# Stage A's low weights: VectorE's difference replaced by an accumulating transfer

## What is computed

```python
h = rmsnorm(x, pre_norm_g[0])
p = h @ w_in                           # (2112, 1024) @ (1024, 3072)
a, g, z = jnp.split(p, 3, axis=-1)
c = a * jax.nn.sigmoid(g)              # then a causal depthwise convolution of 31 taps over c
y = silu(layernorm(conv(c))) * silu(z)
x = x + rmsnorm(y @ w_out, post_norm_g[0])
```

## Time and profile before

| | |
|---|---|
| median of 3 runs | 2333.99 us (2333.13 to 2339.67) |
| the profiled execution | 2334.64 us |
| its span, first to last instruction | 2332.9 us |
| mean granted clock of TensorE | 0.991 |
| stage A in the span | about 24 to 600 us |
| chain that ended last | PE 91%, DMA 3%, DVE 3%, ACT 1%, POOL 1% |
| VectorE, ACT, POOL busy | 1644.4, 921.3, 246.0 us |

### The profile page before, as it was taken

The page is one execution under the profiler, slowest core; times in us unless marked ns, Lnnn a source line. Parts: engine busy times, 40 slices in busy tenths (PEclk is TensorE's granted clock), DMA queues, the critical chain, the costliest instruction groups (busy, mean ns, idle before and its releaser), DMA issues.

```text
span 2332.9 us, 30211 instructions
## 1 busy us (share of the span) xinstructions
PE 2264.9 (97%) x12020; PEld 1972.4 (85%) x12020; DVE 1644.4 (70%) x2044; ACT 921.3 (39%) x1385; POOL 246.0 (11%) x419
## 2 busy tenths in 40 slices
PE   7899999999999998999998999999999999998998
PEld 6788899999888886888886888877879999996885
DVE  5589999997578988989888937742376666665221
ACT  5422222222443224666664115531136565655110
POOL 1100000101221100000000101210110000000000
PEclk9999999999999999999999999999999999999999
DMA  4322333323545313333335335342213232326221
GB/s 168 122 91 93 115 121 135 111 85 120 152 155 180 109 46 110 97 108 118 119 113 227 108 138 213 134 161 80 81 59 103 93 101 95 97 84 247 84 106 37
DMA packets 126075, 275.18 MB, mean 118 GB/s; under 512 B 17136, under 2 KB 53488, under 8 KB 124144
## 3 DMA queue, kind: packets, MB, share of 16 engines
q1 hardware_dynamic: 102448, 194.61, 25.7%
q0 software_dynamic: 23488, 78.64, 8.8%
HBM read 194.82 MB, written 78.75 MB: 117 GB/s over the span
## 4 chain that ended last, share of the span: by engine, by line
PE 91%; DMA 3%; DVE 3%; ACT 1%; issue 1%; POOL 1%; SPq 0%; DVEq 0%; ACTq 0%
PE PS L1966 29%; PE PS L1967 29%; PE PS L1968 29%; PE PS L2164 2%; DMA s_scratch<-m 1%; DMA st<-s_scratch 1%; PE PS L2034 1%; PE PS L2012 1%; DMA yb<-y_scratch 1%; PE PS L1977 1%; DMA raw<-wa_in_in 0%; DVE xn L1376 0%; PE PS L2021 0%; DVE Wbl L1371 0%; DMA xt<-x_in 0%
## 5 line engine op out<-in xcount | busy, mean ns | idle before, releaser
L1405 DVE SCALAR_TENSOR_TENSOR acc<-cp,cw,acc 128x513 f32<-128x513 f32 (+3 forms) x464 | 360.4, 777 | 13.7
L1966 PE MATMUL PS<-HAh,Wh 128*128 128x512 f32 (+2 forms) x960 | 341.5, 356 | 0.1
L1967 PE MATMUL PS<-HAl,Wh 128*128 128x512 f32 (+2 forms) x960 | 339.6, 354 | 0.0
L1968 PE MATMUL PS<-HAh,Wl 128*128 128x512 f32 (+2 forms) x960 | 339.4, 354 | 0.0
L1966 PE MATMUL PS<-Wbh,s7h 128*128 128x512 f32 (+1 forms) x544 | 216.2, 398 | 21.3 <-DVE Wbl L1371 21.3
L1967 PE MATMUL PS<-Wbl,s7h 128*128 128x512 f32 (+1 forms) x544 | 213.9, 393 | 0.0
L1968 PE MATMUL PS<-Wbh,s7l 128*128 128x512 f32 (+1 forms) x544 | 213.5, 392 | 0.0
L1966 PE MATMUL PS<-Vh,HBh 128*128 128x512 f32 (+1 forms) x544 | 212.4, 390 | 0.1
L1967 PE MATMUL PS<-Vl,HBh 128*128 128x512 f32 (+1 forms) x544 | 211.8, 389 | 0.0
L1968 PE MATMUL PS<-Vh,HBl 128*128 128x512 f32 (+1 forms) x544 | 211.7, 389 | 0.0
L1966 PEld LDWEIGHTS PS<-HAh,Wh 128*128 128x128 f32 x960 | 181.2, 189 | 15.5 <-issue 0.5
(11 more groups left out here) (198 smaller groups left out, 5112.4 us busy)
## 6 DMA issues: line engine op xcount, KB each, us to landing
raw<-wa_in_in SPq DMA_DIRECT2D x48, 512.0 KB, 3.6
rawv<-wb_v_in SPq DMA_DIRECT2D x64, 256.0 KB, 4.8
QWr<-wb_uz_in SPq DMA_DIRECT2D x64, 256.0 KB, 2.6
v_scratch<-vb POOLq DMA_DIRECT2D x64, 256.0 KB, 2.6
vt<-v_scratch SPq DMA_DIRECT2D x32, 512.0 KB, 3.7
s_scratch<-m POOLq DMA_DIRECT2D x32, 512.0 KB, 3.8
rawb<-wb_out_in SPq DMA_DIRECT2D x32, 512.0 KB, 5.9
st<-s_scratch SPq DMA_DIRECT2D x14, 1024.0 KB, 4.9
```

The source lines that it names most:

```text
L1405: return nc.vector.scalar_tensor_tensor(out=out, in0=src, scalar=w, in1=first, op0=ALU.mult, op1=ALU.add)
L1966: nc.tensor.matmul(out, wh, xh, start=start, stop=False, skip_group_check=seeded)
L1967: nc.tensor.matmul(out, wh, xl, start=False, stop=False, skip_group_check=seeded)
L1968: return nc.tensor.matmul(out, wl, xh, start=False, stop=stop, skip_group_check=seeded)
```

## The change

VectorE's `a_low` goes. ACT, right after `Wh`, writes `Wl = -Wh` (a second copy with scale -1, which first waits for the one before). POOL then issues a transfer from the weights in DRAM into `Wl` that adds to what is there, so that `Wl` ends as weights minus `Wh`. It has semaphores of its own, one for each of the three buffers, and TensorE waits for those. On POOL the transfers for units 0, 1 and 2 stand behind the powers of tiles 3, 5 and 7, and the one for unit n + 2 behind the powers of turn n of the unit loop, ahead of that turn's stores. SP's load of `raw` stays as it was, so the weights are read twice.

```diff
+        a_lo = [sem(f"a_lo{i}") for i in range(3)]
+        a_hi, a_neg, a_mm, a_sig, a_prod, a_zs = (sem(f"a_{n}") for n in ("hi", "neg", "mm", "sig", "prod", "zs"))
...
+            def a_low(n):
+                pool.wait_ge(a_neg, n + 1)
+                nc.gpsimd.dma_start(kp(Wl[n % 3]), wa_in[n % UNITS_A, :, :], accum_op=ALU.add).then_inc(a_lo[n % 3], 16)
...
             for t in range(9):
                 n1_rsqrt(t)
+                if t in (3, 5, 7):
+                    a_low(t // 2 - 1)
             for n in range(2 * UNITS_A):
                 h, j, m = unit_a(n)
                 for i in (2 * n, 2 * n + 1):
                     if 9 + i < NTILES:
                         n1_rsqrt(9 + i)
+                if 3 <= n + 2 < 2 * UNITS_A:
+                    a_low(n + 2)
                 if m == 1:
                     c_store(JA * h + j)
...
             def a_high(n):
                 act.wait_ge(a_raw[n % 3], 16 * (n // 3 + 1))
                 nc.scalar.activation(kp(Wh[n % 3]), kp(raw[n % 3]), ACT.Copy).then_inc(a_hi, 1)
+
+                act.wait_ge(a_hi, n + 1)
+                nc.scalar.activation(kp(Wl[n % 3]), kp(Wh[n % 3]).bitcast(fp32), ACT.Copy, scale=-1.0).then_inc(a_neg, 1)
...
-            def a_low(n):
-                dve.wait_ge(a_hi, n + 1)
-                split_low(kp(Wl[n % 3]), kp(raw[n % 3]), kp(Wh[n % 3]), a_lo)
...
                 if c == (1 if n < 3 else 0):
-                    if 3 <= n + 2 < 2 * UNITS_A:
-                        a_low(n + 2)
...
                 n1_low(t)
-                if t in (1, 3, 5):
-                    a_low(t // 2)
...
                 if c == 0:
-                    pe.wait_ge(a_lo, n + 1)
+                    pe.wait_ge(a_lo[n % 3], 16 * (n // 3 + 1))
```

More of the change, by code:

```diff
@@ L335, in build @@
         a_raw = [sem(f"a_raw{i}") for i in range(3)]
-        a_hi, a_lo, a_mm, a_sig, a_prod, a_zs = (sem(f"a_{n}") for n in ("hi", "lo", "mm", "sig", "prod", "zs"))
+        a_lo = [sem(f"a_lo{i}") for i in range(3)]
+        a_hi, a_neg, a_mm, a_sig, a_prod, a_zs = (sem(f"a_{n}") for n in ("hi", "neg", "mm", "sig", "prod", "zs"))
         a_cst, a_zst, a_tap, a_conv = (sem(f"a_{n}") for n in ("cst", "zst", "tap", "conv"))
```

## The result

| | before | after |
|---|---|---|
| median | 2335.95 us (4 runs) | 2366.3 us (4 runs, 2362.63 to 2367.07) |
| profiled execution: span | 2332.9 us | 2365.3 us |
| mean granted clock of TensorE | 0.991 | 0.986 |

The ratio is 1.0127, with a 95% interval of 1.0115 to 1.0139: 30 us slower by both, and the sum of the forecast is 29.

What follows compares the result with a forecast made beforehand. Stage A was taken as bound by TensorE from about 105 us, before that by the row-statistics chain. Start delay, transfer waits and clock losses, less old waits, gave +29.1 us on 2334.6: 2364, range 2353 to 2390.

Steps and rivals of the forecast that it cites:

- unit 2, start of chunk 2: Stage A's start: unit 2's transfer, behind tile 7's power, lands at 43.0 against a 38.1 start; +4.9 us, copy's 1.1 included.
- clock behind chunk 2: After the new wait at chunk 2, TensorE restarts at the lower granted clock; +1.7 us, likewise at chunk 6.
- wait at chunk 6: Unit 3's transfer, queued on POOL behind tile 12's power, makes TensorE wait 5.7 + 5.5 - 0.9 = 10.3 us.
- wait at chunk 8: Unit 4's transfer, queued on POOL behind tile 14's power, makes TensorE wait 3.0 + 5.5 = 8.5 us.
- wait at chunk 10: Unit 5's transfer, queued on POOL behind tile 16's power, makes TensorE wait 8.5 us.
- landing L: Adding transfer's time from issue to landing, estimated at 5.5 us from plain transfers; possible from 3.2 to 9.1.
- The 4.4 us: Alternative landing estimate for the 512 KB adding transfer, from the Trainium skill's pages; it would make the sum 4.4 us less.
- the transfer is cheap: Rival: landing about 3.2 us, the waits short, +20 us, 2355; chance 0.82 together with the forecast.
- rival A: Adding transfer much slower than a plain one, above 9 us; 2399 at 12 us; chance 0.13, shared with a split-up add.
- rival B: POOL runs ahead at units 3, 4 and 5 and only old waits go: 2334, at best 2332; chance 0.05.
- ACT's copy: ACT's second copy, about 1.1 us each, costs only at stage A's start, ahead of tile 3's square: +1.1 us.
- the old waits: Waits of 4.2 and 3.1 us before the transposes of tiles 13 and 15 vanish in longer ones; 0.8 comes back.

Runs made afterwards that it cites:

- the reordered queue: The first follow-up: changed kernel with adding transfers for units 0 to 6 moved ahead of powers in POOL's queue; 2346.4 us, ratio 1.0036 to the kernel before.
- the last and fastest kernel: Kernel before with raw loads for units 5, 6 ahead of loads of tiles 14, 16, and first store of c ahead of tile 12's power; 2326.1 us.
- SP's new order: Kernel before with SP's loads of raw for units 5 and 6 issued ahead of the loads of tiles 14 and 16; 2329.4 us, ratio 0.9971.

## Why the prediction was right

It was right in sign and mechanism: four waits for the adding transfer, at the chunks and behind the powers that it names. The time came out within 3 us (2366.3 against 2364), and that is in part luck, as the table shows. Times are counted from the first transposes, which start at 9.80 in the execution after and at 8.35 in the one before, 1.45 us later, as gpre landed after 6.7 us there and 5.3 here:

| step | predicted | traced |
|---|---|---|
| VectorE's difference gone | 0 | 0 (0.9999 with it alone) |
| unit 0: start of the first chunk | +1.1 | 26.13 - 23.78 - 1.45 = +0.9 |
| unit 2, start of chunk 2 | +4.9 | 45.34 - 38.10 - 1.45 = +5.8 |
| clock behind chunk 2 | +1.7 | 9.93 - 7.24 = +2.7 |
| wait at chunk 6 | 10.3 | 10.27 |
| clock behind it | +1.7 | 22.64 - 9.93 - 10.27 = +2.4 |
| tile 13: old wait, what comes back | -4.2, +0.8 | -4.2, +0.63 |
| wait at chunk 8 | 8.5 | 8.69 |
| tile 15: old wait | -3.1 | -3.3 |
| wait at chunk 10 | 8.5 | 8.70 |
| clock behind chunks 8 and 10, over that of before | 0 | +0.5, +0.7 |
| sum at the transposes of tile 16 | +29.1 | 139.68 - 105.29 - 1.45 = +32.9 |
| landing L | 5.5 | 5.6 |

(9.93, 7.24 and 22.64 are the differences of the two timelines at 72.57 and 62.64, at 45.34 and 38.10, and at 91.62 and 68.98.) Rows of the kernel before and then of the kernel after, for chunk 0 and the end of the stretch:

```profile
30.10 1.91 PE L1977 MATMUL PS<-con,xn 128*128 128x128 f32 x16
...
68.98 1.03 PE L1977 MATMUL PS<-con,xn 128*128 128x128 f32 x8
...
105.29 0.70 PE L1977 MATMUL PS<-con,xn 64*128 64x64 f32 x8
```
```profile
33.77 1.91 PE L1981 MATMUL PS<-con,xn 128*128 128x128 f32 x16
...
139.68 0.71 PE L1981 MATMUL PS<-con,xn 64*128 64x64 f32 x8
```

So the sum was 3.8 us short in the stretch that it describes, the later start added 1.45, and some 2 us were given back behind stage A (34.4 us at tile 16, 32.4 in the spans), 1.6 of them in the wait for y_scratch, 1.0 for 2.6. Together they leave the difference of the spans 3 us from the sum, and that of the medians, 30.3, 1 us.

**The waits** at chunks 6, 8 and 10 came out within 0.2 us each, because their first part could be read before: the place in POOL's queue from a store that stood there already. The landing was a luckier sum. 4.3 for a plain transfer and 1.3 for twice the bytes make 5.6; measured are 3.8 for the plain one and 1.8 for the add, 5.6 as well. The 4.4 us that stands beside it in the prediction as an estimate, with the 4.4 us lower sum, is not what the trace shows: 5.6 decides. The range's lower part (the transfer is cheap) was excluded by the landing of 5.6, rival A by the same, rival B by the four waits. VectorE's busy time fell by 52.5 us and not by 59, ACT's rose by 50.8.

**Chunk 2** came 0.9 us later than the sum had it, and more than that is in chunk 0: it takes 33.77 - 26.13 = 7.64 us in the kernel after and 30.10 - 23.78 = 6.32 before. Its matmuls start 0.43 us apart at first and 0.23 later on; after ten such gaps in one trace and after three in the other. The change is not shown to be the reason. The same count is 0 with ACT's copy alone, 3 in the reordered queue and 9 in the last and fastest kernel. The windows show a granted clock of 1.00 there all the same.

**The clock** was under-sized, at 1.7 us for a restart. Windows of the kernel after behind chunk 6:

```profile
84.00:86.00 2.00, 2.00 (x5) 1.61 (x6) 0.00 (x0) 0.00 (x0) 0.00 (x0) 0.50 1.02 416
86.00:88.00 2.00, 2.00 (x6) 1.52 (x6) 0.00 (x0) 1.28 (x1) 0.00 (x0) 0.50 0.92 279
88.00:90.00 2.00, 2.00 (x9) 1.66 (x8) 0.00 (x0) 0.00 (x0) 0.00 (x0) 0.86 0.44 178
```

1.0 + 1.0 + 0.3 = 2.3 us. The 1.7 was read off one execution, and one is not enough: TensorE's wait of 8.12 us for sz (at 910.72 in the trace of before) is the same to 0.01 us in ten of the eleven traces, and the windows behind it show 1.7 us (with the plain transfer) to 3.1 (in the kernel after) lost at the lower level, 1.2 GHz; the kernel before has 2.8. A price for a restart that is read off one row can be off by over 1 us.

**ACT's copy** was the step with the weakest reasoning, though it hardly moved the sum. "It costs where ACT is in the chain, which is at the start: +1.1" is right only because the waits for Wl cover the rest; the copies in the turns of chunks 5 and 6 had been counted in the 5.7 and the 7.1, as they should. By itself the copy, with the difference waiting for it, costs 5 to 6 us. The same is true of the old waits: I took 4.2 and 3.1 off as given back, which is right, and concluded for the first experiment that they would come back in part, which is wrong; they came back in full and with the copy on top (5.7 and 4.2, and 5.7 and 3.3 with the copy alone). The changed kernel was predicted well because its own waits were the longest in the stretch; the kernels between it and the one before weren't.

## What to carry to other kernels

A transfer or a store in a queue that works in program order is as late as the latest thing ahead of it: ask for each item what it waits for, and whether the items behind need that too. Read the lateness of a new item off an old one in the same place. Before a wait is explained by what the change adds, look whether the same wait is in the kernel before and what it hangs on. And where several waits lie in one stretch, remove the first and look again, since taking the longest away may only uncover the next.

## What the runs showed of the hardware

- An adding transfer of 512 KB into SBUF issued by POOL lands after 5.6 us, a plain one in the same place after 3.8; issuing takes POOL 849 to 1211 ns (median 877) with the add and 528 to 782 (540) without.
- It lengthens its neighbours: POOL's stores of c take 4.1 us from issue to landing (median) in the kernel after against 3.2, those of silu(z) 5.7 against 4.3. With the plain transfer they are 4.0 and 4.8, so the store of c is slowed by a transfer of either kind. TensorE waited for none of it in the steady part; ACT's waits for raw weights there rose from 36.0 to 51.2 us.
- A restart of TensorE costs 1.7 to 3.1 us at the lower level behind one and the same wait of 8.12 us in ten traces. The length of the wait alone doesn't tell whether the clock falls: in the kernel before, a wait of 2.58 us that ends at 1235.26 left it at 1.00 in the windows behind it, and one of 2.59 us that ends at 619.32 is followed by 0.50; in the kernel with SP's new order it is 1.00 behind 2.17 us (79.33) and 0.55 behind 2.23 us (2115.60).
- Executions of one kernel differ by 3 to 9 us from the fastest to the slowest. The first transposes start between 8.35 and 10.51 us in the traces of this study, and chunk 0 has 0 to 10 of the gaps of 0.43 us, at 0.2 us each.
